# Second layer of a mixture-of-experts block: the largest expert moved to the end, its outputs spread to their tokens by 0/1 products, the other rows gathered beside it, empty slots skipped in the gathers

## What is computed

```python
g_top = top_k(softmax(h @ w_group + b_group), 1)      # one of 4 groups
e_top = top_k(e_logits[g_top], 2)                     # two of its 4 experts, with weights e_w
y[slot] = (silu(x[slot] @ w_gate[e]) * (x[slot] @ w_up[e])) @ w_down[e]
h = h + mod_5 * sum over the token's two slots of e_w * y[slot]
```

## Time and profile before

| | us |
|---|---|
| median of 3 runs | 1981.47 |
| lowest, highest | 1977.7, 1984.41 |
| the profiled execution: time, span | 1981.44, 1979.6 |
| busy in the span: PE, DVE, ACT, POOL | 1826.1, 796.3, 569.5, 68.1 |

### The profile page before, as it was taken

How to read it: one execution, slowest core, us unless ns; L and a number is a source line. 1 busy time by engine, 2 the same in 40 slices (tenths; PEclk the granted TensorE clock), 3 DMA queues, 4 the chain that set the end, 5 groups by cost and what they waited for, 6 DMA issues and landing times.

```text
span 1979.6 us, 37745 instructions
## 1 busy us (share of the span) xinstructions
PE 1826.1 (92%) x16354; PEld 1170.0 (59%) x16354; DVE 796.3 (40%) x1717; ACT 569.5 (29%) x1225; POOL 68.1 (3%) x68
## 2 busy tenths in 40 slices
PE   5999999889889989999998999999899897999964
PEld 3554668667654655555554765467667685555532
DVE  3424456678821451011111541356778525111112
ACT  3113233557620321111110523232557423100000
POOL 0000000000010000000001000000000100000001
PEclk8999999999989999999999999999899998999987
DMA  9611100092150787778999412001000316999996
GB/s 380 235 57 43 33 29 25 20 301 85 50 215 34 282 317 293 271 295 304 391 341 352 165 36 98 10 23 54 6 17 1 130 43 228 346 394 393 363 400 230
DMA packets 153413, 360.70 MB, mean 182 GB/s; under 512 B 11800, under 2 KB 74400, under 8 KB 152992
## 3 DMA queue, kind: packets, MB, share of 16 engines
q1 hardware_dynamic: 130128, 316.33, 43.1%
q0 software_dynamic: 6640, 23.60, 3.7%
q10 hardware_dynamic: 16480, 18.36, 2.6%
HBM read 317.89 MB, written 40.37 MB: 181 GB/s over the span
## 4 chain that ended last, share of the span: by engine, by line
PE 79%; DVE 9%; DMA 5%; ACT 4%; issue 1%; SPq 1%; POOL 0%; ACTq 0%; POOLq 0%; DVEq 0%
PE ps L1410 16%; PE ps L990 15%; PE ps L1433 8%; PE ps L1272 7%; PE ps L975 6%; PE ps L1100 4%; PE ps L1134 3%; DMA arena<-in_moe_w_gu 3%; PE ps L1166 2%; PE ps L1158 2%; PE ps L935 1%; PE ps L1391 1%; DMA arena<-in_w_mod 1%; DVE att_small L2212 1%; PE ps L1470 1%
## 5 line engine op out<-in xcount | busy, mean ns | idle before, releaser
L1410 PE MATMUL ps<-arena 128*32 128x256 f32 x6080 | 348.9, 382 | 9.6 <-DMA arena<-in_moe_w_gu 6.5
L990 PE MATMUL ps<-arena 128*128 128x256 f32 (+2 forms) x1056 | 348.9, 486 | 0.9 <-ACT arena L1682 0.9
L1410 PEld LDWEIGHTS ps<-arena 128*32 128x32 f32 x6080 | 200.5, 111 | 140.2 <-issue 10.6
L990 PEld LDWEIGHTS ps<-arena 128*128 128x128 f32 x1056 | 198.9, 191 | 130.4 <-issue 116.2
L2625 DVE TENSOR_TENSOR arena<-ps,arena 128x128 f32<-128x128 f32 x95 | 27.7, 292 | 420.9 <-ACT arena L1916 420.9
L1433 PE MATMUL ps<-arena 128*32 128x256 f32 x3040 | 183.1, 382 | 0.0
L1272 PE MATMUL ps<-arena 128*128 128x256 f32 (+1 forms) x512 | 143.4, 434 | 2.0 <-DVE arena L2310 2.0
L1916 ACT ACTIVATE arena<-ps 128x128 f32<-128x128 f32 x95 | 26.4, 278 | 376.6 <-PE ps L1410 376.6
L1100 PE MATMUL ps<-arena 32*128 32x256 f32 (+5 forms) x528 | 130.4, 508 | 3.1 <-ACT arena L1756 2.3
L1807 ACT ACTIVATE arena<-ps,att_small 128x768 f32<-128x768 f32 (+2 forms) x160 | 123.3, 773 | 24.3 <-DVE att_small L2212 23.2
L1433 PEld LDWEIGHTS ps<-arena 128*32 128x32 f32 x3040 | 89.4, 109 | 61.2 <-issue 1.0
(11 more groups left out here) (371 smaller groups left out, 2074.4 us busy)
## 6 DMA issues: line engine op xcount, KB each, us to landing
arena<-in_moe_w_gu SPq DMA_DIRECT2D x32, 4096.0 KB, 20.3
arena<-in_moe_w_down SPq DMA_DIRECT2D x32, 2048.0 KB, 12.5
arena<-in_w_mod SPq DMA_DIRECT2D x24, 2048.0 KB, 18.3
y_rows<-zeros_t SPq DMA_DIRECT2D x2, 9216.0 KB, 51.9
arena<-in_w_in SPq DMA_DIRECT2D x6, 2048.0 KB, 7.9
arena<-in_w_in SPq DMA_DIRECT2D x8, 1024.0 KB, 5.7
y_rows<-arena ACTq DMA_DIRECT2D x80, 96.0 KB, 8.0
arena<-in_w_out SPq DMA_DIRECT2D x4, 1536.0 KB, 9.1
```

What stands on the lines that cost most here:

```text
L990: last = pe.matmul(PS[:, 4 + k % 2, 0:ch[2]], aT[:, c, t * P:(t + 1) * P], wbuf[:, j % 2, c, 0:ch[2]], start=(c == 0), stop=(c == DC - 1))
L1410: last = pe.matmul(PS[32 * q:32 * q + 32, 2 + g % 2, 0:2 * P], xT(item_par(L, k))[:, a:a + SUB], gate_up_cols(ring_e(L, r), c, q), start=( ...
```

## The change

- `ORDER` becomes one list per layer; in the second layer rank 0 is moved from position 2 to the last, 14 (`LAST`). The positions then have 3 blocks (0 to 8), 2 blocks (9 to 13) and 3 blocks (14).
- The last item isn't stored. The down products of the item before are done at its first block (`g == end`), and the last item's down product is done once for all 96 slots, as two halves of 512 columns. VectorE multiplies each half with the modulation, now also kept as a row over 128 partitions (`gate_row`, made in the routing stage by eight more products and a copy of 128x1024). A 0/1 matrix `last_oh` of slots by tokens then spreads each half to the four tiles, eight products; VectorE adds each with the token's weight (`last_w`, zero for tokens without a slot there) to its tile.
- `last_tokens` on VectorE makes these weights and the matrix; tokens of the last item get in `dest` the place of a row of zeros.
- The eight gathers wait only for the stores of the other items. Tiles 0 and 1 are summed by VectorE (`rows_sum`) ahead of each half's modulation; tiles 2 and 3 are scaled by ScalarE and added by GpSimd (two additions of 128x1024 each). Output is written in eight halves of 256 KB.
- All row gathers, in both layers, get a bounds check that skips row N. Five fills are added ahead of the residual tiles.

```diff
-ORDER = list(range(RANKED, EXP)) + list(range(RANKED - 1))
+ORDER = [list(range(RANKED, EXP)) + list(range(RANKED - 1)), list(range(RANKED, EXP)) + list(range(1, RANKED - 1)) + [0]]
...
-    r = [(pos, i, min(P, RANK_CAP[L][k] - i * P) // SUB) for pos, k in enumerate(ORDER) for i in range(-(-RANK_CAP[L][k] // P))]
-    first = [next(n for n, it in enumerate(r) if it[0] == ORDER.index(k)) if k in ORDER else len(r) for k in range(EXP)]
+    r = [(pos, i, min(P, RANK_CAP[L][k] - i * P) // SUB) for pos, k in enumerate(ORDER[L]) for i in range(-(-RANK_CAP[L][k] // P))]
+    first = [next(n for n, it in enumerate(r) if it[0] == ORDER[L].index(k)) if k in ORDER[L] else len(r) for k in range(EXP)]
...
+        LAST = NI[1] - 1
+        LAST_N = SUB * ITEMS[1][LAST][2]
+        LAST_G = first_sub(1, LAST)
+        LAST_AT = [(i, half) for half in range(2) for i in range(3)]
+        LAST_AT = LAST_AT[:6] + [(3, 0), (3, 1)]
+        LAST_BANK = [0, 1, 2, 3, 4, 7, 5, 6]
...
+        gate_row = rows[:, 0:D]
+        last_oh = ar(M_X + 4 * D + 6 * P, 4 * P).rearrange("p (t n) -> p t n", t=NT - CT)
+        last_hT = ar(M_X + 4 * D + 10 * P, FC * LAST_N).rearrange("p (c n) -> p c n", c=FC)
+        LAST_ZERO = SUB * ITEMS[1][0][2]
+        last_w = ss[:, 36:36 + NT]
...
-            for i in range(NT - CT):
-                sp.wait_ge(S("tok_d"), NT + i + 1)
-                sp.dma_start(out[0, i * P:(i + 1) * P, :], restok[:, i, :]).then_inc(S(f"f_out{i % 2}"), 16)
+            for n, (i, half) in enumerate(LAST_AT):
+                a, b = half * 512, half * 512 + 512
+                sp.wait_ge(S("tok_d"), NT + n + 1)
+                sp.dma_start(out[0, i * P:(i + 1) * P, a:b], restok[:, i, a:b]).then_inc(S(f"f_out{n % 2}"), 16)
             for q in range(2):
-                sp.wait_ge(S(f"f_out{q}"), 16 * (NT // 2 + NT - CT))
+                sp.wait_ge(S(f"f_out{q}"), 16 * (NT // 2 + OTN[1] // 2 + NT - CT))
...
                 if L == LAYERS - 1:
+                    fill_clock(5)
...
+                        pe.matmul(PS[:, c // 4, (c % 4) * P:(c % 4 + 1) * P], bc(g, (0, P)), ident, start=True, stop=True,
+                                  skip_group_check=True)
...
                             h_transpose(g - 1)
-                        if g > ga + 1:
+                        if ga + 1 < g < end + 1:
                             down(g - 2)
+                        if g == end:
+                            down(g - 1)
+
+                def scattered_last():
+                    h_transpose(NS[L] - 1)
+                    wd = down_w(ring_e(L, it[LAST][0]))
+                    pe.wait_ge(S("hT_ev"), g0 + NS[L])
+                    pe.wait_ge(S(f"wd_in{ring_e(L, it[LAST][0]) % 2}"), 16 * slot_loads(2, L, it[LAST][0]))
+                    pe.wait_ge(S("y_a"), g0 + end)
+                    for half in range(2):
+                        for c in range(FC):
+                            last = pe.matmul(PS[0:LAST_N, 5 + half, :], last_hT[:, c, :], wd[:, c, half * 512:(half + 1) * 512],
+                                             start=(c == 0), stop=(c == FC - 1))
+                        last.then_inc(S("dn_ps"), 1)
+                    pe.wait_ge(S("diag_ready"), 2)
+                    for n, (i, half) in enumerate(LAST_AT):
+                        pe.wait_ge(S("y_a"), g0 + end + (2 if LAST_BANK[n] == 6 else 1 + half))
+                        pe.matmul(PS[:, LAST_BANK[n], :], last_oh[0:LAST_N, i, :],
+                                  ysb(item_par(L, LAST))[0:LAST_N, half * 512:(half + 1) * 512], start=True, stop=True).then_inc(S("comb_ps"), 1)
...
-                    last_ones(NS[L])
+                    scattered_last()
...
                     act.wait_ge(S("ftok_ps"), OT0[L] + OTN[L] + 3)
+                    act.activation(gate_row, PS[:, 0:2, :].rearrange("p b n -> p (b n)"), ACT.Copy)
...
                 experts(L)
+            for i in range(2, NT - CT):
+                act.wait_ge(S(f"g_in{i}"), 32 * ((NT + 3 - i) // 4 + 1))
+                for k in (1, 0):
+                    n = k * NT + CT + i
+                    act.activation(y_pair(i, k), y_pair(i, k), ACT.Copy, scale=wtok[:, n:n + 1]).then_inc(S("tok_a"), 1)
...
+                end = LAST_G if L == LAYERS - 1 else NS[L]
...
+                    if g >= end:
+                        a = SUB * (g - end)
+                        dve.tensor_copy(last_hT[:, :, a:a + SUB], PS[:, 4 + 3 * (g % 2), 0:P].rearrange("p (c s) -> p c s", c=FC)
+                                        ).then_inc(S("hT_ev"), 1)
+                        return
...
+                def last_tokens():
+
+                    t0 = CT
+                    dw = dest[:, :].rearrange("p (k t) -> p k t", k=TOPK)[:, :, t0:]
+                    m, sel, w, z = [ss[:, 12 * j:12 * j + 12].rearrange("p (k t) -> p k t", k=TOPK)[:, :, t0:] for j in (0, 1, 2, 4)]
+                    link(dve.tensor_scalar(m, dw, float(P * LAST), None, ALU.is_ge))
+                    link(dve.scalar_tensor_tensor(out=sel, in0=dw, scalar=float(P * (LAST + 1)), in1=m, op0=ALU.is_lt, op1=mul))
+                    dve.tensor_scalar(z, dw, -1.0, float(LAST_ZERO), mul, ALU.add)
+                    link(dve.tensor_tensor(w, sel, wtok[:, :].rearrange("p (k t) -> p k t", k=TOPK)[:, :, t0:], mul))
+                    link(dve.tensor_tensor(z, z, sel, mul))
+                    dve.tensor_tensor(last_w[:, t0:], w[:, 0, :], w[:, 1, :], ALU.add)
+                    dve.tensor_tensor(dw, dw, z, ALU.add)
+                    at = ss[:, 64:64 + NT - CT]
+                    for i in range(NT - CT):
+                        last = dve.tensor_scalar(at[:, i:i + 1], slots[:, LAST:LAST + 1], -float((CT + i) * P), None, ALU.add)
+                    link(last)
+                    dve.tensor_tensor(last_oh, bc(K[:, C_BLK:C_BLK + 1], (0, NT - CT), (1, P)), bc(at, (1, NT - CT), (0, P)), ALU.is_equal
+                                      ).then_inc(S("diag_ready"), 1)
...
+                    last_tokens()
...
-                        if L == LAYERS - 1 and g > ga + 1:
+                        if L == LAYERS - 1 and ga + 1 < g < end + 1:
                             y_gated(g - 2)
+                        if g == end:
+                            y_gated(g - 1)
...
                     run(TAIL_I[L], gt, NS[L])
-                    last_ones(NS[L])
+                    h_evac(NS[L] - 1)
+                    par = item_par(L, LAST)
+                    for i in range(2):
+                        rows_sum(i)
+                        a, b = 512 * i, 512 * i + 512
+                        dve.wait_ge(S("dn_ps"), g0 + end + i + 1)
+                        dve.wait_ge(S(f"y_out{par}"), 16 + 16 * stores(L, par, LAST))
+                        dve.tensor_tensor(ysb(par)[0:LAST_N, a:b], PS[0:LAST_N, 5 + i, :], gate_row[0:LAST_N, a:b], mul).then_inc(S("y_a"), 1)
+
+            def rows_sum(i):
+                t = CT + i
+                dve.wait_ge(S("ftok_a"), OT0[1] + OTN[1] + i + 1)
+                dve.wait_ge(S(f"g_in{i}"), 32 * ((NT + 3 - i) // 4 + 1))
+                o = restok[:, i, :]
+                link(dve.scalar_tensor_tensor(out=o.rearrange("p (c n) -> p c n", n=P), in0=y_pair(i, 1).rearrange("p (c n) -> p c n", n=P),
+                                              scalar=wtok[:, NT + t:NT + t + 1], in1=residual(t), op0=mul, op1=ALU.add))
+                link(dve.scalar_tensor_tensor(out=o, in0=y_pair(i, 0), scalar=wtok[:, t:t + 1], in1=o, op0=mul, op1=ALU.add))
...
                     combine()
-            for i, t in enumerate(out_tiles(1)):
-                dve.wait_ge(S("ftok_a"), OT0[1] + OTN[1] + i + 1)
-                dve.wait_ge(S(f"g_in{i}"), 32 * ((NT + 3 - i) // 4 + 1))
-                o = restok[:, i, :]
-                link(dve.scalar_tensor_tensor(out=o.rearrange("p (c n) -> p c n", n=P), in0=y_pair(i, 1).rearrange("p (c n) -> p c n", n=P),
-                                              scalar=wtok[:, NT + t:NT + t + 1], in1=residual(t), op0=mul, op1=ALU.add))
-                dve.scalar_tensor_tensor(out=o, in0=y_pair(i, 0), scalar=wtok[:, t:t + 1], in1=o, op0=mul, op1=ALU.add
+            for n, (i, half) in enumerate(LAST_AT):
+                if i >= 2:
+                    dve.wait_ge(S("mix_done"), LAYERS + 2 * (i - 1))
+                dve.wait_ge(S("comb_ps"), NT + n + 1)
+                o = restok[:, i, half * 512:(half + 1) * 512]
+                dve.scalar_tensor_tensor(out=o, in0=PS[:, LAST_BANK[n], :], scalar=last_w[:, CT + i:CT + i + 1], in1=o, op0=mul, op1=ALU.add
...
-                        in_offset=bass.IndirectOffsetOnAxis(ap=slots[0:n, k:k + 1], axis=0)).then_inc(S(f"xg_in{item_par(L, k)}"), 16)
+                        in_offset=bass.IndirectOffsetOnAxis(ap=slots[0:n, k:k + 1], axis=0),
+                        bounds_check=N - 1, oob_is_err=False).then_inc(S(f"xg_in{item_par(L, k)}"), 16)
...
-                    pool.wait_ge(S(f"y_out{k}"), 16 + 16 * stores(L, k, NI[L]))
```

(12 more changed lines are left out.)

13 lines of the change are left out of this document (8 added, 5 removed).

## The result

The changed kernel takes 1985.76 us in the median (1981.42 to 1993.12, 20 runs), the kernel before 1978.65 beside it (1973.84 to 1984.52, 20 runs). The ratio is 1.0036, 95% interval 1.0025 to 1.0047: 7.1 us slower (5 to 9), 0.36%. The forecast was 1977.0 with a range of 1972.0 to 1983.0. The profiled execution of the changed kernel took 1990.64 us with a span of 1988.8, 4.9 above its own median.

What follows compares the result with a forecast made beforehand. TensorE bound the second layer's expert stage up to 1860 us, afterwards the order in which weights can be asked for. First gather -9.2, end +3.8 and routing +1.0 gave -4.4: 1981.4 to 1977.0 us, range 1972.0 to 1983.0.

Steps and rivals of the forecast that it cites:

- A: Second layer's routing, with added fills, gate products and row copy: +1.0 us taken, from -0.5 to +3.0.
- 16 passes at 0.136 us is 2.2: Routing: eight added gate products over 128 rows, priced per pass from eight passes taking 1.09 us.
- Rival 4: Clock falls in the gate block and again in the 0/1 products: routing +3.0, products 1.5, total 1980.5 us; chance 0.08.
- B: Second layer's expert order and weight loads: the last gate/up load lands 5.6 us earlier, at 1931.5 plus the routing term.
- the lull: Second layer's expert stage, 1860 to 1870: DMA share falls to 0.69, missing 2.0 MB, 4.9 us at 409 GB/s.
- Rival 2: The DMA gap at 1860 to 1870 isn't closed, last gate/up load not earlier: price 5.6, 1982.6 us; chance 0.12.
- No wait for weights arises before the lull: Expert stage: position 11's gate/up load is issued 22 us ahead of use, and its 4.2 MB take 10.
- The bound on the gathers: Row gathers, both layers: skipping empty slots costs nothing, bounds 0 to +1 us each; other gathers have 15 us of cover.
- Part 3: Last expert: three blocks, 15.1 us on TensorE from its weights, then ScalarE's signal; first gather 9.2 us earlier, less routing.
- meanwhile: Last expert: ScalarE signals only behind the last silu, so gathers run beside the last down products alone.
- Part 4: From first gather to the end: gathers, scaling, four GpSimd adds, last sums, output; 26.4 us against 22.6, +3.8.
- G: Start of the first of the eight final gathers, forecast at 1947.8 us plus the routing term.

Runs made afterwards that it cites:

- e3: The changed kernel with its eight wide gate products first and the eight narrow ones behind them, not in turn: 1982.38 us, ratio 1.0015.
- e9: The kernel before with only five clock fills added ahead of the second layer's residual products: 1976.30 us, ratio 0.9988.
- e2: The kernel before with only the second layer's order changed, rank 0 last, its rows still stored and gathered: 1981.98 us, ratio 1.0016.
- e7: The changed kernel with ScalarE's signal that all rows are stored raised right behind the store of the last item but one: 1986.77 us, ratio 1.0041.

## Why the prediction was wrong

The sum said -4.4 us. With its own terms beside what was measured: A +1.0 against +4.4 (mean of six +4.8); nothing in the first layer against +2.5; landing -5.6 against -2.5; the last expert's part -3.6 (9.2 less 5.6) against -3.8; the end +3.8 against +6.0. The errors are +3.4, +2.5, +3.1, -0.2 and +2.2, and -4.4 plus 11.0 is the +6.6 of the rows.

**Part 1, A: the price of the added products.** The step "16 passes at 0.136 us is 2.2" failed. The passes by themselves are cheap: grouped, all 32 took 2.64 (e3), less than 2.2 and the 1.11 of the earlier trace rows together (the 1.11 stood at clock 0.50; at full clock the sixteen narrow passes take 0.66), and R is then 0.7 below before, not 1.0 above. What it left out is that each stands between two narrow ones. The rows it drew on (8 passes in 1.09) are runs of equal shapes. The kernel before does have two widths in turn, in every block, around the transpose that the prediction puts at 0.26:

```profile
1946.55 0.33 PE L1420 MATMUL ps<-consts,arena 128*128 128x128 f32 x1
...
1946.82 1.93 PE L1433 MATMUL ps<-arena 128*32 128x256 f32 x32
```

One wide pass between narrow ones takes 0.27 from its start to the next product's, twice the 0.136 of a pass among its like. The sum used the 0.26 and didn't read it as a price of the alternation. The term for the fills was right: they fit, the first pair fell from 3.68 to 1.97, and with the alternation gone R is 2.5 us below before (e9). Rival 4, the clock falling in the gate block, was a real case and bigger than its price: A is then +8.2, not +3.0, since all 32 passes, the fills and the second pair pay.

**Part 2, B: the lull.** The mechanism held in its first steps: position 9's down products and SP's wait come one block earlier, the load behind goes out 5.5 us earlier, the DMA share is 1.03. Rival 2 was wrong. The step that failed is the last one, that behind a closed lull the landing moves with the issue. A lull gives back at most the transfer time that was missing in it: by the forecast's own row 0.34 of ten us, 3.4 us (the 4.9 came from bytes at 409 GB/s, while the full stretch in its place reaches only 373), and I then took 5.6, more than either, with "the skipped rows widen it". 1.1 to 2.6 arrived. "No wait for weights arises before the lull" failed beside it: the load for position 11 was given 10 us and 22 of cover, but such loads took 26.4 us in the kernel before (1835.10 to 1861.55) and 27.4 in e2, and TensorE waited for it.

**The bound on the gathers, costed at nothing.** The reason given (all but the first gather have 15 us of cover) was right for what it spoke of, the gathers' own length: 0.957 us in the median for 0.912. It did not ask what the longer program does elsewhere on GpSimd, in the first layer too. The 2.5 us are outside both bounds (0 to +1).

**Part 3** held: first gather 16.06 behind the landing against 16.3 (1947.8 less 1931.5), released by ScalarE's signal as said. e7 shows what the sentence about "meanwhile" had in it: by the rows that signal's place is worth 4.4 us.

**Part 4: the end.** Its chain was right to the last link, the sizes were not. Tile 2's rows were there at G+12.9, not 12.4; ScalarE's pass of 1.14 (1.02 taken) let the first add start at G+14.2, not 13.6; four adds took 9.6 to the end of the last, not 8.5 (2.35 each, 2.1 taken, between the row's 1.90 and the scaled 2.3 of the earlier trace rows, of which the second was the right one); the output took 3.4 behind the last sum, not 2.9. Together 2.2. The Trainium skill's figure for an add of 2048 elements (GPSIMD Engine Reference, Performance versus the Vector engine) would have given an estimate of 2.25, nearer to the 2.35 than mine. The 0/1 products hid as forecast.

**The range.** Its upper end of 1983.0 was drawn from rivals that move one term at a time. Here four terms were off, each by more than 2 us and in the same direction, and what was measured lies outside the bounds that A (-0.5 to +3.0) and the bound on the gathers (0 to +1) had been given. That the rows' +6.6 comes within 0.5 us of the +7.1 is in part luck: the rows are of one execution, and the twenty lie 12 us apart.

## What to carry to other kernels

Before a product is put into a loop of products of another width, look at what the alternation costs there (0.25 us for each change in this kernel's gate block) and group by width. A gap in the transfers was worth at most the transfer time missing in it here, and less arrived, however much earlier the next load is issued. An instruction added to a queue can cost at a place that the diff doesn't touch, so compare all stages of the two traces, the first layer's too, and measure from landmarks, because single executions differ by more than such a change.
